# Feed-forward up projections with the high and low activations as one moving operand of 512 columns

## What is computed

```python
def swiglu_ffn(h, w_gate_up, w_down):          # once, D_FF = 2816
    gu = h @ w_gate_up
    return (jax.nn.silu(gu[..., :D_FF]) * gu[..., D_FF:]) @ w_down
...
x = x + jnp.square(jax.nn.relu(hf @ ffn_w1[layer])) @ ffn_w2[layer]   # twice, D_FF_2 = 4096
```

## Time and profile before

| what | value |
|---|---|
| median of 3 runs | 889.83 us (888.96 to 889.91) |
| profiled execution, its own time | 890.11 us |
| its span | 888.0 us |
| TensorE busy | 870.8 us, 98% of the span |
| mean granted TensorE clock | 0.992 of full speed |

### The profile page before, as it was taken

One profiled execution on the slowest core, in us unless ns is written; L12 is line 12 of the kernel. 1 busy time (PEld: TensorE's weight loads), 2 busy tenths in 40 slices (PEclk: granted clock), 3 DMA queues, 4 the chain that ended last, 5 costly groups with the idle time before them and its releaser, 6 DMA issues.

```text
span 888.0 us, 14246 instructions
## 1 busy us (share of the span) xinstructions
PE 870.8 (98%) x5828; PEld 786.4 (89%) x5828; DVE 531.3 (60%) x576; ACT 432.5 (49%) x587; POOL 44.8 (5%) x104
## 2 busy tenths in 40 slices
PE   8999999999999799999999999999999999999997
PEld 8888899999999799888999999989867999999996
DVE  5865555444446579577675555567676765555553
ACT  6466444434435367743554444436465374444431
POOL 2100100000000200220000000003000000000000
PEclk9999999999999799999999999999999999999999
DMA  9724055555555574336675555434611575555511
GB/s 314 283 93 138 29 192 187 189 189 189 173 190 171 180 223 134 118 96 217 197 242 190 188 189 188 137 130 116 218 36 50 191 238 192 189 188 187 190 45 47
DMA packets 98441, 147.68 MB, mean 166 GB/s; under 512 B 4042, under 2 KB 81938, under 8 KB 98402
## 3 DMA queue, kind: packets, MB, share of 16 engines
q1 hardware_dynamic: 97234, 143.11, 49.3%
q0 software_dynamic: 1120, 4.00, 1.5%
q10 hardware_dynamic: 48, 0.02, 0.0%
HBM read 146.05 MB, written 1.05 MB: 166 GB/s over the span
## 4 chain that ended last, share of the span: by engine, by line
PE 92%; DVE 4%; ACT 2%; POOL 1%; issue 1%; DVEq 0%; POOLq 0%; ACTq 0%
PE bank L1785 27%; PE bank L1786 27%; PE bank L1787 27%; DVE w_lo L1119 1%; PE bank L1859 1%; PE bank L2398 1%; PE bank L2421 1%; PE bank L2383 1%; PE bank L2377 1%; PE bank L1987 1%; ACT x_norm L672 1%; PE bank L1999 1%; PE bank L1986 1%; PE bank L2152 0%; PE bank L2124 0%
## 5 line engine op out<-in xcount | busy, mean ns | idle before, releaser
L1119 DVE TENSOR_TENSOR w_lo<-w_raw,w_hi 128x2048 fp32r<-128x2048 f32 (+2 forms) x129 | 289.7, 2252 | 153.6 <-ACT w_hi L643 153.4
L1785 PE MATMUL bank<-xT_hi,w_hi 128*128 128x256 f32 x1068 | 303.7, 284 | 0.0
L1787 PE MATMUL bank<-xT_hi,w_lo 128*128 128x256 f32 x1068 | 302.1, 283 | 0.0
L1786 PE MATMUL bank<-xT_lo,w_hi 128*128 128x256 f32 x1068 | 302.1, 283 | 0.0
L643 ACT ACTIVATE w_hi<-w_raw 128x2048 fp32r<-128x2048 f32 (+2 forms) x129 | 241.4, 1879 | 90.8 <-PE bank L1787 83.0
L1785 PEld LDWEIGHTS bank<-xT_hi,w_hi 128*128 128x128 f32 x1068 | 203.9, 191 | 4.4 <-issue 2.4
L1786 PEld LDWEIGHTS bank<-xT_lo,w_hi 128*128 128x128 f32 x1068 | 204.0, 191 | 1.9 <-issue 0.2
L1787 PEld LDWEIGHTS bank<-xT_hi,w_lo 128*128 128x128 f32 x1068 | 204.0, 191 | 0.2
L1785 PE MATMUL bank<-w_hi,ff_hi 128*128 128x512 f32 x344 | 134.4, 391 | 0.0
L1786 PE MATMUL bank<-w_lo,ff_hi 128*128 128x512 f32 x344 | 134.3, 390 | 0.0
L1787 PE MATMUL bank<-w_hi,ff_lo 128*128 128x512 f32 x344 | 133.8, 389 | 0.0
(11 more groups left out here) (248 smaller groups left out, 699.0 us busy)
## 6 DMA issues: line engine op xcount, KB each, us to landing
w_raw<-in_ffn_w SPq DMA_DIRECT2D x64, 1024.0 KB, 5.3
w_raw<-in_ffn_w_gate_up SPq DMA_DIRECT2D x22, 1024.0 KB, 5.1
w_raw<-in_ab_w_in SPq DMA_DIRECT2D x12, 1024.0 KB, 5.4
w_raw<-in_ffn_w_down SPq DMA_DIRECT2D x11, 1024.0 KB, 4.7
w_raw<-in_swa_w_in SPq DMA_DIRECT2D x5, 1024.0 KB, 11.3
w_raw<-in_swa_w_out SPq DMA_DIRECT2D x4, 1024.0 KB, 7.7
w_raw<-in_ab_w_out SPq DMA_DIRECT2D x4, 1024.0 KB, 5.9
w_raw<-in_c_w_out SPq DMA_DIRECT2D x4, 1024.0 KB, 5.2
```

The costliest lines, as they stand in the source:

```text
L1119: dve.tensor_tensor(view(w_lo, ch), view(w_raw, ch), view(w_hi, ch).bitcast(F32), ALU.subtract).then_inc(S["lo_done"], 1)
L1785: pe.matmul(out, sh, mh, start=first, stop=False)
L1786: pe.matmul(out, sh, ml, start=False, stop=False)
L1787: return pe.matmul(out, sl, mh, start=False, stop=last)
```

## The change

`feature_stacked` takes the place of `feature_major` in all feed-forward phases. The operands xT_hi and xT_lo become the two halves of one tile, so that one matmul of 512 columns multiplies both by w_hi; a second matmul of 256 columns adds xT_hi by w_lo. A chunk is 32 matmuls in place of 48 and fills two banks: in each bank columns 0 to 255 hold the main sum, columns 256 to 511 the cross term. VectorE adds the halves of both banks with a `tensor_reduce` over pairs. In ffn1 this is done once for the gate (ahead of Silu) and once for the up projection (ahead of the product). In ffn2 VectorE sums, then makes max(s, 0) times s in one instruction; ScalarE no longer reads PSUM there and only rounds to ff_hi. For the last slice of each phase VectorE and ScalarE work on half the features at a time. `hidden2` no longer makes ff_lo: that is `hidden_low2`, which in the entrance of an ffn2 phase stands behind `low` of c5. The transposes of ffn2's first slice go to bank 1 in place of bank 2, and TensorE's ffn2 loop has one round fewer, written out behind it. The lists of the engines keep their order but for what is shown.

```diff
-        xT_hi = sb("xT_hi", [P, NT, KT, P], F32R)
-        xT_lo = sb("xT_lo", [P, NT, KT, P], F32R)
+        xT = sb("xT", [P, KT, 2, NT, P], F32R)
+        xT_hi = xT[:, :, 0].rearrange("p k t c -> p t k c")
+        xT_lo = xT[:, :, 1].rearrange("p k t c -> p t k c")
...
+            return psum[:, b + fs.start:b + fs.stop].rearrange("p f (s c) -> p f c s", s=2)
...
+            def feature_stacked(ch, b, between=None, first=None):
+                hi, lo = view(w_hi, ch), view(w_lo, ch)
+                for f in range(2):
+                    if f == 1 and between:
+                        between()
+                    for k in range(KT):
+                        pe.matmul(bank[b + f], hi[:, k, f * P:(f + 1) * P], xT[:, k].rearrange("p s t c -> p (s t c)"),
+                                  start=k == 0, stop=False)
+                        last = pe.matmul(bank[b + f][:, 0:SEQ], lo[:, k, f * P:(f + 1) * P],
+                                         xT[:, k, 0].rearrange("p t c -> p (t c)"), start=False, stop=k == KT - 1)
+                    if f == 0 and first:
+                        last.then_inc(S[first], 1)
+                last.then_inc(S["mm_done"], 1)
...
-                relu_square(f, c[1], 1, 1)
+                hidden_high2(f, 1, 1)
                 high_upto(c[5].index + 1)
...
+            def hidden_high2(f, i, buf, it=0):
+                act.wait_ge(S["ff2_h"], (N2 + 1) * f + i + 1 + 2 * it)
+                act.activation(ff_hi[buf][:], ff_h[:], ACT.Copy).then_inc(S["ff2_hi"], 1)
...
+            def gate_sum(ch, i, it=0):
+                dve.wait_ge(S["mm_done"], ch.index + 1 + 3 * it)
+                dve.tensor_reduce(ff_g[:], main_and_cross(0), axis=AX, op=ALU.add).then_inc(S["ff1_gs"], 1)
...
+                dve.tensor_reduce(ff_g[:], main_and_cross(2), axis=AX, op=ALU.add).then_inc(S["ff1_us"], 1)
+                dve.wait_ge(S["ff1_us"], i + it)
+                dve.tensor_tensor(ff_h[:], ff_act[:], ff_g[:], ALU.mult).then_inc(S["ff1_h"], 1)
...
+            def last_hidden(ch):
+                dve.wait_ge(S["ff1_sg"], N1)
+                for f, fs in enumerate(EACH):
+                    if f == 0:
+                        dve.wait_ge(S["ff1_first"], 1)
+                    else:
+                        dve.wait_ge(S["mm_done"], ch.index + 1)
+                    dve.tensor_reduce(ff_g[:, fs], main_and_cross(2, fs), axis=AX, op=ALU.add).then_inc(S["ff1_us"], 1)
+                    dve.wait_ge(S["ff1_us"], N1 - 1 + f)
+                    dve.tensor_tensor(ff_h[:, fs], ff_act[:, fs], ff_g[:, fs], ALU.mult).then_inc(S["ff1_h"], 1)
+                for f, fs in enumerate(EACH):
+                    dve.wait_ge(S["ff1_hi"], N1 + f)
+                    dve.tensor_tensor(ff_lo[1][:, fs], ff_h[:, fs], ff_hi[1][:, fs].bitcast(F32),
+                                      ALU.subtract).then_inc(S["ff1_lo"], 1)
...
             for ch in c[-3:]:
                 low(ch)
-            hidden(c[-3], N1 - 1, buf=1)
+            gate_sum(c[-4], N1 - 1)
+            last_hidden(c[-3])
...
+            def hidden2(f, ch, i, it=0):
+                b = 2 * (i % 2)
+                dve.wait_ge(S["mm_done"], ch.index + 1 + 4 * it)
+                dve.tensor_reduce(ff_g[:], main_and_cross(b), axis=AX, op=ALU.add).then_inc(S["ff2_sum"], 1)
+                dve.wait_ge(S["ff2_sum"], N2 * f + i + 2 * it)
+                dve.scalar_tensor_tensor(out=ff_h[:], in0=ff_g[:], scalar=0.0, in1=ff_g[:], op0=ALU.max,
+                                         op1=ALU.mult).then_inc(S["ff2_h"], 1)
+            def hidden_low2(f, i, buf, it=0):
+                dve.wait_ge(S["ff2_hi"], (N2 + 1) * f + i + 1 + 2 * it)
+                dve.tensor_tensor(ff_lo[buf][:], ff_h[:], ff_hi[buf][:].bitcast(F32), ALU.subtract).then_inc(S["ff2_lo"], 1)
...
                 low_upto(c[4].index + 1)
-                hidden2(f, 1, 1)
+                hidden2(f, c[1], 1)
                 low_upto(c[5].index + 1)
+                hidden_low2(f, 1, 1)
                 squared_factor((4, 6)[f])
```

More of the change, by code:

```diff
@@ L205, in build @@
         squares = take(P, NT, DM)
+        ff_g = take(P, 2, SEQ)
         used[0] = 0
@@ L964, in squared_relu @@
                 high_upto(c[-2].index + 1)
-                relu_square(f, c[-5], N2 - 2, 0)
+                hidden_high2(f, N2 - 2, 0)
                 high_upto(c[-1].index + 2)
-                relu_square(f, c[-3], N2 - 1, 1)
+                for part, fs in enumerate(EACH):
+                    act.wait_ge(S["ff2_h"], (N2 + 1) * f + N2 + part)
+                    act.activation(ff_hi[1][:, fs], ff_h[:, fs], ACT.Copy).then_inc(S["ff2_hi"], 1)
                 high_upto(c[-1].index + 1 + after)
@@ L1361, in hidden, with hidden_low @@
+            def hidden_low(i, it=0):
                 dve.wait_ge(S["ff1_hi"], i + 1 + it)
-                dve.tensor_tensor(ff_lo[buf][:], ff_h[:], ff_hi[buf][:].bitcast(F32), ALU.subtract).then_inc(S["ff1_lo"], 1)
-            def first_hidden_low(high, count, ready):
+                dve.tensor_tensor(ff_lo[0][:], ff_h[:], ff_hi[0][:].bitcast(F32), ALU.subtract).then_inc(S["ff1_lo"], 1)
+            def last_hidden(ch):
[8 more added lines that the diff above has]
+                    dve.tensor_tensor(ff_h[:, fs], ff_act[:, fs], ff_g[:, fs], ALU.mult).then_inc(S["ff1_h"], 1)
+                for f, fs in enumerate(EACH):
+                    dve.wait_ge(S["ff1_hi"], N1 + f)
+                    dve.tensor_tensor(ff_lo[1][:, fs], ff_h[:, fs], ff_hi[1][:, fs].bitcast(F32),
+                                      ALU.subtract).then_inc(S["ff1_lo"], 1)
@@ L1365, in first_hidden_low @@
+            def first_hidden_low(high, count, ready, b=2):
                 dve.wait_ge(S[high], count)
-                dve.tensor_tensor(ff_lo[0][:], bank[2][:].rearrange("p (a b) -> p a b", a=2),
+                dve.tensor_tensor(ff_lo[0][:], bank[b][:].rearrange("p (a b) -> p a b", a=2),
                                   ff_hi[0][:].bitcast(F32), ALU.subtract).then_inc(S[ready], 1)
@@ new lines, in hidden_low2, with last_hidden2 @@
+            def hidden_low2(f, i, buf, it=0):
+                dve.wait_ge(S["ff2_hi"], (N2 + 1) * f + i + 1 + 2 * it)
+                dve.tensor_tensor(ff_lo[buf][:], ff_h[:], ff_hi[buf][:].bitcast(F32), ALU.subtract).then_inc(S["ff2_lo"], 1)
+            def last_hidden2(f, ch):
+                for part, fs in enumerate(EACH):
+                    if part == 0:
+                        dve.wait_ge(S["ff2_first"], f + 1)
+                    else:
+                        dve.wait_ge(S["mm_done"], ch.index + 1)
+                    dve.tensor_reduce(ff_g[:, fs], main_and_cross(2, fs), axis=AX, op=ALU.add).then_inc(S["ff2_sum"], 1)
+                    dve.wait_ge(S["ff2_sum"], N2 * f + N2 - 1 + part)
+                    dve.scalar_tensor_tensor(out=ff_h[:, fs], in0=ff_g[:, fs], scalar=0.0, in1=ff_g[:, fs], op0=ALU.max,
+                                             op1=ALU.mult).then_inc(S["ff2_h"], 1)
+                for part, fs in enumerate(EACH):
+                    dve.wait_ge(S["ff2_hi"], (N2 + 1) * f + N2 + part)
+                    dve.tensor_tensor(ff_lo[1][:, fs], ff_h[:, fs], ff_hi[1][:, fs].bitcast(F32),
+                                      ALU.subtract).then_inc(S["ff2_lo"], 1)
@@ L1885, in whole, with hidden_transposes @@
                 feature_major(ch, dst, **more)
-            def hidden_transposes(ready, count, done):
+            def hidden_transposes(ready, count, done, b=2):
                 def blocks():
@@ L2232, in squared_relu @@
                 up2(c[5], 1)
-                with pe.Fori(0, N2 // 2 - 2) as it:
+                with pe.Fori(0, N2 // 2 - 3) as it:
                     down2(f, c[6], 2, 0, it)
@@ L2237, in squared_relu @@
                     up2(c[9], 1, it)
+                down2(f, c[-6], N2 - 4, 0)
+                up2(c[-5], 0)
+                down2(f, c[-4], N2 - 3, 1)
+                up2(c[-3], 1, first="ff2_first")
                 for t in range(NT):
```

102 lines of the change are left out of this document (53 added, 49 removed).

## The result

The changed kernel takes 896.42 us (median of 4 runs, 896.31 to 896.54) against 889.87 us (888.96 to 889.97) for the kernel before: ratio 1.0076, 95% interval 1.0064 to 1.0088. It is slower by 0.76%, 6.7 us above the forecast and outside its range. The profiled execution took 896.31 us with a span of 894.6; the one before took 890.11 with 888.0.

The account below looks back on a forecast made before the run. TensorE, busy in 98% of the span, was taken as the bound. ffn1 -1.0, ffn2a +0.4 + 0.05 and ffn2b +0.4 gave -0.15 on 890.11, so 889.96, as a median 889.7 us; overall range 886.8 to 893.4.

Parts of the forecast that it names:

- The saving: Stacked chunks in all feed-forward phases: 12.5 ns less per group of three matmuls, 10.0 us in all if nothing waits.
- rival E: The stacked matmul does not do what it says, for instance by a lower granted clock; no chance of its own.
- The entrances: Start of ffn2a and ffn2b: TensorE waits 3.4 us ahead of down c4, net +0.4 us in each phase.
- Slice 2's ff_lo: Entrance of ffn2a, after the rope angles: ready at 453.7, wanted at 453.9, so 0.2 us of slack.
- The exit of ffn1: End of ffn1: next chunk's low part starts 2.6 us later, 3.6 saved ahead of it, net -1.0 us.
- The sum: VectorE's added reduction of 1024 PSUM elements to 512 results: 1.225 us, or 1.27 with the semaphore.
- B: The sum costs 1.76 us because results and operands don't overlap: 3.0 us slower, 892.7 us; chance 0.17.
- C: The sum costs only 0.69 us: five times 0.54 less, 887.0 us; chance 0.12.
- The steady loops: Loops of ffn1 and ffn2: VectorE's added work lies under TensorE, at cost zero.
- the exits of ffn2: End of the ffn2 phases: ScalarE's next high part 0.4 us later, +0.05 us in ffn2a, nothing in ffn2b.
- Rival A: Nothing is saved per matmul, a stacked one costs 240 ns: 8.9 us slower, 898.7 us; chance 0.08.
- D: The engines' lists don't bind and all added work hides: -10.0 us, 879.8 us; chance 0.04.

## Why the prediction was wrong

**The saving: wrong.** The step that failed is "3 x 120.0 = 360.0 becomes 227.5 + 120.0 = 347.5 ns". Both spacings came from runs of equal matmuls; in turn they cost 352.8. That saves 7.2 ns per pair instead of 12.5, 5.8 us instead of 10.0: 4.2 us of the miss. The grouped order gives 347.5, so the single prices hold for runs of one size, and adding them for sizes in turn was the mistake. The prediction said that no row has a 512 and a 256 in turn, but allowed only 1.5 ns either way. The Trainium skill's rule of a fixed cost of about 2.5 ns per warm matmul (TensorE: Matmul & The Clock Gate, "Wait — 56ns, not 53.3ns?") would have made the saving an estimated 2.0 us. The trace disagrees: the measured 5.8 lies between the two, and the grouped 10.0 is the rows' figure.

**The clock: missing.** The second step that failed is a term put at nothing, in rival E: "The granted clock was 1.00, and nothing here lowers it" was read in a stretch where TensorE never idles, while the same text gives TensorE two new idle stretches of 3.4 us. The price was in the trace of before, at the exit of ffn1, where TensorE idles for x_norm. The stretch around it, before and after (the third number from the end is the clock):

```profile
293.00:304.00 11.00, 7.93 (x36) 7.56 (x37) 5.87 (x10) 3.84 (x11) 3.55 (x7) 0.53 0.36 112
```

```profile
293.00:304.00 11.00, 6.29 (x31) 5.85 (x32) 6.87 (x12) 4.85 (x15) 3.65 (x7) 0.69 0.43 136
```

The trace has the clock at half there for 10.24 us before and for 6.83 after. A wait at an entrance should have been priced as wait plus half clock: 1.7 and 1.55 us, 3.25 of the miss. The Trainium skill warns that idle gaps between bursts of matmuls bring the lower clock back (the same page, "Why this matters for your kernels"), and that the moment at which the clock changes varies from run to run ("What's actually happening"). The traces agree with the first and go beyond the second: after 3.07 us of idle time the half clock came in one execution of the changed kernel and not at all in another.

**The entrances: right.** The forecast had c4 start 3.0 later than before; it starts 3.24 later in ffn2a, 3.05 of it gained within the phase. The wait was forecast at 3.4 and is 3.07 in the row, which counts from the end of the last matmul, or 3.2 from where the next one could have started, 439.9. That is 0.4 later than forecast: 0.2 from a phase that starts later, 0.1 from the slower pairs and the down chunk between them, and 0.1 from a slip in the sum (24 pairs at 12.5 ns save 0.3, so TensorE would be ready at 439.6 and not 439.5). Slice 2's ff_lo, called just in time, ends at 453.86 (forecast 453.7); the half clock gave it room, and where the subtraction was moved ahead, without the wait before it, it was late.

**The exit of ffn1: right.** Forecast +2.6 and a hidden wait of about 1.0; measured: TensorE, done with the transposes and entering the next phase, starts again at 298.04 before and 299.02 after, which is 0.98 later. Slice 9's sum starts at 267.52, where its product started at 269.15; counted from the phase's start, which is 0.04 later, that is 1.67 earlier. So the exit itself cost 0.98 + 1.63 = 2.61, with a saving ahead of it of 1.67 in place of the forecast 3.6; that is the slower pairs again. The wait for the last slice is 0.79, the one ahead of up c30 1.26 where 1.5 was forecast.

**The sum: right.** 1.22 us, priced at 1.225; rivals B and C are out. Max-and-multiply was priced 0.75 and took 0.69. The steady loops hide it all, and the exits of ffn2 show nothing else.

**Rival A** (nothing saved per matmul) had the right sign for the wrong size: a pair would cost 360, it costs 352.8. D fails on the order of the statements and on that of the matmuls; the version with both changed reaches its figure of 879.8 within 0.4 us.

The miss adds up: 4.2 for the pairs, 3.25 for the half clocks, 0.4 for ffn1's down chunks (5.50 us instead of 5.47; in the grouped order they are back at 5.47, so this too goes with the alternating order), less 0.8 that is absorbed between the exit of ffn1 and ffn2a, about half of it where the clock stayed low for a shorter time, and less 0.4 outside the span (1.7 us around it, 2.1 before): 6.65, against 6.7 measured.

## What to carry to other kernels

Price a stream of matmuls from rows of the same mix and the same order; where sizes differ, issue them in runs of two or more of one size, and check the sum of single prices on one row. Where a change puts a wait on TensorE, even one of 2 to 3 us, charge it twice: once for the wait and once for the half clock that may follow it. If work in a hand-written order moves from one engine to another, walk through both engines' lists at every entrance and exit, and put the work that TensorE needs next ahead of the work for later chunks: here that and the grouped order together took less than twenty lines and turned 0.76% slower into 1.07% faster.

## What was not expected of the hardware

- A single matmul of 256 or 512 columns between matmuls of the other size makes the stream some 4 ns longer (an estimate from one chunk each); a strictly alternating stream costs 5.3 ns more per pair (352.8 against 347.5 ns). There it is the 512 that takes longer (235.8 against 226.7 ns), while the 256 is cheaper (116.7 against 120.0). Runs of two are enough to avoid the cost: an up and a down chunk take 11.01 us with them and 11.03 with runs of eight.
- A half-clock stretch of 3.41 us followed an idle TensorE of 3.07 us in some executions and not in others of the same kernel, and once followed 2.14 us. With thirteen unused matmuls in the idle time the clock stayed at 1.00 in the trace that was taken, and no execution took longer than 893.83 us, the fastest without them.
- The 12 to 14 ns that a matmul costs beyond its columns are there only at full clock. At half clock, behind the exit of ffn1 in the kernel before, matmuls of 256 columns start 0.213 us apart, which is one column a cycle at 1.2 GHz and nothing else. By that a stretch of 3.41 us holds 8 matmuls of 512 columns, 1.8 us' worth at full clock, and costs 1.6 us (an estimate; measured 1.55 and 1.7):

```profile
300.10 0.41 PE L1785 MATMUL bank<-w_hi,xT_hi 128*128 128x256 f32 x1
...
300.74 0.41 PE L1785 MATMUL bank<-w_hi,xT_hi 128*128 128x256 f32 x1
```

- A reduction that reads 1024 elements out of PSUM and writes 512 costs 1.22 us, the same as one that writes 4: what is read sets the price.
